# Expert gates of a mixture layer: one product of 256 columns per token, sums added by VectorE, steps of eight tokens

## The reference, cut to what matters

```
expert_idx = take_along_axis(cand_idx, best_c)        # (T, 8, 16): first key * 128 + second key
gates = softmax(best_s)
u = take(expert_u, ib);  act = gelu(einsum('td,thkd->thk', xb, u))
w = gb * act
v = take(expert_v, ib);  out = einsum('thk,thkd->td', w, v)
```

## Time and profile before

| | |
|---|---|
| median of 3 runs | 3182.61 us (3180.1 to 3184.99) |
| the profiled execution | 3179.26 us, its span 3177.4 us |
| mean granted TensorE clock | 0.994 of full speed |
| TensorE busy | 3115.6 us (98%) |
| GpSimd busy | 2335.9 us (74%) |
| VectorE busy | 1830.0 us (58%) |
| ScalarE busy | 767.3 us (24%) |

### The profile page before, as it was taken

How to read it: one execution, slowest core, us unless ns; L and a number is a source line. 1 busy time by engine, 2 the same in 40 slices (tenths; PEclk the granted TensorE clock), 3 DMA queues, 4 the chain that set the end, 5 groups by cost and what they waited for, 6 DMA issues and landing times.

```text
span 3177.4 us, 41446 instructions
## 1 busy us (share of the span) xinstructions
PE 3115.6 (98%) x14250; PEld 2523.3 (79%) x14250; DVE 1830.0 (58%) x2659; ACT 767.3 (24%) x1253; POOL 2335.9 (74%) x1127
## 2 busy tenths in 40 slices
PE   8999999999999999999999999999999998899998
PEld 6788777788888888888888888888888775578886
DVE  6488645221255566665764266767676667776621
ACT  3244123220122222222323111111111255332201
POOL 6833654677776888888888788888888763278876
PEclk9999999999999999999999999999999999899999
DMA  3211211223322344344444666666666421022222
GB/s 143 93 51 50 100 66 53 79 99 119 108 96 95 130 182 174 144 156 176 173 169 172 235 190 189 190 191 186 185 185 188 144 78 45 27 90 96 99 92 73
DMA packets 245547, 405.71 MB, mean 128 GB/s; under 512 B 145600, under 2 KB 145728, under 8 KB 244160
## 3 DMA queue, kind: packets, MB, share of 16 engines
q1 hardware_dynamic: 224560, 331.68, 32.0%
q10 hardware_dynamic: 20880, 72.62, 5.9%
HBM read 335.04 MB, written 69.21 MB: 127 GB/s over the span
## 4 chain that ended last, share of the span: by engine, by line
PE 93%; DVE 4%; POOL 1%; issue 1%; ACT 1%; DMA 0%; POOLq 0%; SPq 0%; ACTq 0%; DVEq 0%
PE bank L598 23%; PE bank L600 23%; PE bank L599 23%; PE banks L598 2%; PE banks L600 2%; PE banks L599 2%; PE banks L747 1%; PE bank L812 1%; PE bank L713 1%; PE bank L711 1%; PE bank L712 1%; PE bank L895 1%; PE banks L896 1%; PE bank L896 1%; PE banks L895 1%
## 5 line engine op out<-in xcount | busy, mean ns | idle before, releaser
L500 POOL TENSOR_TENSOR w_hi<-w_raw,ones 128x1024 fp32r<-128x1024 f32 x492 | 956.0, 1943 | 731.9 <-PE bank L600 581.3
L502 POOL TENSOR_TENSOR w_lo<-w_raw,w_hi 128x1024 fp32r<-128x1024 f32 x492 | 1231.6, 2503 | 38.6
L598 PE MATMUL bank<-h_hi,w_hi 128*128 128x512 f32 x2176 | 864.1, 397 | 9.6 <-DVE h_lo L1878 7.0
L600 PE MATMUL bank<-h_hi,w_lo 128*128 128x512 f32 x2176 | 848.1, 390 | 0.0
L599 PE MATMUL bank<-h_lo,w_hi 128*128 128x512 f32 x2176 | 847.2, 389 | 0.0
L598 PEld LDWEIGHTS bank<-h_hi,w_hi 128*128 128x128 f32 x2176 | 408.8, 188 | 105.0 <-DVE h_lo L1878 13.9
L600 PEld LDWEIGHTS bank<-h_hi,w_lo 128*128 128x128 f32 x2176 | 408.4, 188 | 86.8
L599 PEld LDWEIGHTS bank<-h_lo,w_hi 128*128 128x128 f32 x2176 | 409.0, 188 | 82.3 <-issue 2.4
L2343 DVE TENSOR_TENSOR ew_lo<-expert_w,ew_hi 128x512 fp32r<-128x512 f32 x128 | 249.1, 1985 | 182.3 <-ACT ew_hi L1585 178.5
L598 PE MATMUL bank<-ew_hi,w_hi 128*128 128x512 f32 x768 | 303.2, 395 | 0.0
L600 PE MATMUL bank<-ew_hi,w_lo 128*128 128x512 f32 x768 | 303.0, 395 | 0.0
(11 more groups left out here) (443 smaller groups left out, 4390.6 us busy)
## 6 DMA issues: line engine op xcount, KB each, us to landing
w_raw<-weights SPq DMA_DIRECT2D x494, 512.0 KB, 3.2
acts<-act_out_stage ACTq DMA_DIRECT2D x128, 256.0 KB, 2.6
gates<-gate_stage ACTq DMA_DIRECT2D x8, 4096.0 KB, 13.2
acts_in<-acts SPq DMA_DIRECT2D x128, 256.0 KB, 4.3
gates_in<-gates SPq DMA_DIRECT2D x128, 256.0 KB, 4.6
resid<-x SPq DMA_DIRECT2D x4, 512.0 KB, 7.9
resid<-x ACTq DMA_DIRECT2D x4, 512.0 KB, 7.9
out<-final SPq DMA_DIRECT2D x3, 512.0 KB, 2.7
```

Source lines behind the costliest of these rows:

```text
L500: nc.gpsimd.tensor_tensor(w_hi[:, pair, :], w_raw[:, slot, :], one_col.to_broadcast((P, 1024)), ALU.mult).then_inc(hi_split, 1)
L502: nc.gpsimd.tensor_tensor(w_lo[:, pair, :], w_raw[:, slot, :], f32(w_hi[:, pair, :]), ALU.subtract).then_inc(split_done, 1)
L598: mm(out_, hi, rhs_hi, start=first, stop=False)
L600: return mm(out_, lo, rhs_hi, start=False, stop=last)
```

## The change

The two parts of the gate lie side by side in one tile, `hot1[..., 0, :]` and `hot1[..., 1, :]`, and a token is **one product of 256 columns** in place of two of 128. Its two halves of the result are no longer added by TensorE. ScalarE copies the first half to a new tile `gate_part`, VectorE adds the second half, which it reads from the bank, and writes the sum to `gate_stage` (`gates_summed`, L2301 of the changed kernel).

A batch of 4 tokens now needs two banks, so a **step is 2 batches, 8 tokens** (`HOTS` = 2): 64 steps, 8 to a lot, 16 to a block. `LOT_TILES` now gives the tiles of each single step, one or two. In the first three blocks the steps of one tile are step 3, 11 and 14 of the 16. In the last block the row of steps is 1 1 2 1 1 2 1 2, then 2 1 1 2 1 1 1 1. The number of tiles among the steps is 108 as before. VectorE's pieces of the choice are cut anew: five rows in parts 1 and 2, four and two rows in parts 4 and 5, `choose` in halves in parts 6 and 7, `places` in part 9, `picked` in 10 and 12, `chosen_gates` in 13.

```
-LOT_TILES = (4, 4, 4, 4, 3, 3, 3, 2)
+LOT_TILES = ((2, 2, 2, 1, 2, 2, 2, 2), (2, 2, 2, 1, 2, 2, 1, 2)) * 3 + ((1, 1, 2, 1, 1, 2, 1, 2), (2, 1, 1, 2, 1, 1, 1, 1))
-HOTS = 4
+HOTS = 2
...
-    hot1 = place("hot1", [P, HOTS, TOKENS_PER_BATCH, NKEYS], A0 + 56 * KB, F32R)
-    hot1_lo = place("hot1_lo", [P, HOTS, TOKENS_PER_BATCH, NKEYS], A0 + 24 * KB, F32R)
+    hot1 = place("hot1", [P, HOTS, TOKENS_PER_BATCH, 2, NKEYS], A0 + 56 * KB, F32R)
...
+    gate_part = place("gate_part", [P, HOTS, TOKENS_PER_BATCH, NKEYS], S1 + 12 * KB + 64)
...
         for step in range(TT * LOTS * STEPS):
-            n = LOT_TILES[step // STEPS]
-            early = min(n, 3)
-            splits(early)
-            tile += early
+            n = LOT_TILES[step // STEPS][step % STEPS]
+            splits(n)
+            tile += n
             for p in range(HOTS if step + 1 < TT * LOTS * STEPS else 0):
                 gate_batch(step + 1, p)
-                if p == 0:
-                    splits(n - early)
-                    tile += n - early
...
                 for t in range(TOKENS_PER_BATCH):
-                    mm(bank[2 + p][:, t * P:t * P + P], hot2[:, p, t, :], hot1[:, p, t, :], start=t == 0, stop=False)
-                    ins = mm(bank[2 + p][:, t * P:t * P + P], hot2[:, p, t, :], hot1_lo[:, p, t, :],
-                             start=False, stop=t == TOKENS_PER_BATCH - 1)
+                    of = (t % 2) * 2 * NKEYS
+                    ins = mm(bank[2 + 2 * p + t // 2][:, of:of + 2 * NKEYS], hot2[:, p, t, :], hot1[:, p, t].rearrange("p a k -> p (a k)"),
+                             start=t % 2 == 0, stop=t % 2 == 1)
                 ins.then_inc(batch_done, 1)
...
-                fn_at(stage[:, :, bass.ds(t0, TOKENS_PER_BATCH)].rearrange("p k t -> p t k"),
-                      bank[2 + p][:].rearrange("p (t k) -> p t k", k=NKEYS), ACT.Copy).then_inc(gate_read, 1)
+                fn(gate_part[:, p], gate_sums[p][:, :, 0, :], ACT.Copy).then_inc(gate_copied, 1)
...
+        def gates_summed(step):
+
+            if step % STEPS == 0 and step:
+                dve.wait_ge(gates_out, 16 * (step // STEPS))
+            for p in range(HOTS):
+                first = (step % STEPS * HOTS + p) * TOKENS_PER_BATCH
+                dve.wait_ge(gate_copied, c.due(gate_copied))
+                tt_(stage[:, :, first:first + TOKENS_PER_BATCH].rearrange("p k t -> p t k"), gate_sums[p][:, :, 1, :], gate_part[:, p],
+                    ALU.add).then_inc(gate_read, 1)
...
             one_hots(step + 1)
+            gates_summed(step)
             if tt + 1 < TT:
```

More of the change, by code:

```diff
@@ L274, in build @@
     bank += [df_banks[:, 0, :], df_banks[:, 1, :]]
-    bank += [nc.alloc_psum_tensor(f"bank{n}", [P, T], F32) for n in range(4, 8)]
+    banks45 = nc.alloc_psum_tensor("banks45", [P, 2, T], F32)
+    bank += [banks45[:, 0, :], banks45[:, 1, :]]
+    bank += [nc.alloc_psum_tensor(f"bank{n}", [P, T], F32) for n in range(6, 8)]
+    gate_sums = [pair[:].rearrange("p b (t part k) -> p (b t) part k", part=2, k=NKEYS) for pair in (df_banks, banks45)]
     gates = nc.dram_tensor("gates", (T // STAGED_TOKENS, NKEYS, NKEYS, STAGED_TOKENS), F32, kind="Internal").ap()
@@ L300, in build @@
         "hi_split", "split_done", "hot_gated"))
-    choices_here = sem("choices_here")
+    choices_here, gate_copied = (sem(n) for n in ("choices_here", "gate_copied"))
     tile_done, sq_used, lev_done, far_done, o_done = (sem(n) for n in (
@@ L515, in gate_batch @@
             gate = gates_t[:, first:first + TOKENS_PER_BATCH]
-            nc.gpsimd.tensor_tensor(hot1[:, p], f32(hot1[:, p]), gate.unsqueeze(2).to_broadcast((P, TOKENS_PER_BATCH, NKEYS)),
-                                    ALU.mult).then_inc(hot_gated, 1)
+            nc.gpsimd.tensor_tensor(hot1[:, p, :, 0, :], f32(hot1[:, p, :, 0, :]),
+                                    gate.unsqueeze(2).to_broadcast((P, TOKENS_PER_BATCH, NKEYS)), ALU.mult).then_inc(hot_gated, 1)
         tile = START["experts"]
@@ L903, in _, with mixed, twos @@
         tiles_fm(LEAD_TILES - TURN_AT, h_hi, h_lo, acc_read_act)
-        for lot in range(TT * LOTS):
[L906 to L917, removed]
-            else:
-                c.repeat(STEPS - 1, lambda i: mixed())
-                mixed(0, next_choices)
-        tiles_fm(NKEYS - LEAD_TILES - LOT_BATCHES // HOTS * sum(LOT_TILES), h_hi, h_lo, acc_read_act)
+        def mixed(n, first, next_choices=0):
+            gate_batches()
+            for k in range(n):
+                p = (first + k) % 2
+                pe.wait_ge(acc_read_act, c.due(acc_read_act, 1, back=2))
+                tile_fm(p, h_hi, h_lo, bank[p][:])
+                if k == 0 and next_choices:
+                    turn(next_choices)
+        def twos(n, first):
+            c.repeat(n, lambda i: mixed(2, first))
+        tile = LEAD_TILES
+        for lot in range(TT * LOTS):
+            first = tile % 2
+            if lot >= LOTS * (TT - 1):
+                for n in LOT_TILES[lot]:
+                    mixed(n, tile % 2)
+                    tile += n
+                continue
+            twos(3, first)
+            mixed(1, first)
+            if lot % LOTS == LOTS - 1:
+                twos(2, 1 - first)
+                mixed(1, 1 - first, (lot + 1) // LOTS)
+                mixed(2, first)
+            else:
+                twos(4, 1 - first)
+            tile += sum(LOT_TILES[lot])
+        tiles_fm(NKEYS - tile, h_hi, h_lo, acc_read_act)
         pe.wait_ge(gate_read, c.due(gate_read, 0))
@@ L1556, in _ @@
         for lot in range(TT * LOTS):
[L1557 to L1563, removed]
+            for step in range(STEPS):
+                gate_batches()
+                if step == STEPS - 1:
                     act.wait_ge(gate_read, c.due(gate_read, LOT_BATCHES))
@@ L1566, in mixed @@
                                   stage[:].rearrange("p a t -> p (a t)")).then_inc(gates_out, 16)
-                for k in range(n):
-                    key_act(i * n + (key + k), (i * n + k) % 2)
-                    if share and k == 1:
+                for k in range(LOT_TILES[lot][step]):
+                    key_act(key, key % 2)
+                    key += 1
+                    if lot % LOTS == 1 and lot + 1 < TT * LOTS and step == 0 and k == 1:
                         shares()
[L1571 to L1575, removed]
+        c.due(gates_out, 16 * TT * LOTS)
         key_acts(key, NKEYS - key - 2)
@@ L2222, in choose_halves, with choose @@
             dve.wait_ge(dve_step, c.due(dve_step, 3))
-        def choose():
-            best16([(cand[:, h, :], best_s[:, h, :], best_u[:, h * TOPK:h * TOPK + TOPK]) for h in range(PEER_HEADS)])
+        def choose(first=0, end=PEER_HEADS):
+            best16([(cand[:, h, :], best_s[:, h, :], best_u[:, h * TOPK:h * TOPK + TOPK]) for h in range(first, end)])
+            if end < PEER_HEADS:
+                return
             ve.tensor_copy(denom[:, 0, :], best_s[:, :, 0]).then_inc(dve_step, 1)
@@ L2320, in _ @@
             one_hots(step + 1)
+            gates_summed(step)
             if tt + 1 < TT:
[L2322 to L2326, removed]
+                if part in (1, 2, 4, 5):
+                    choose_halves(tt + 1, *{1: (0, 5), 2: (5, 10), 4: (10, 14), 5: (14, 16)}[part])
+                elif part == 6:
+                    choose(0, PEER_HEADS // 2)
+                elif part == 7:
+                    choose(PEER_HEADS // 2)
+                elif part == 9:
                     places(tt + 1)
-                    picked(tt + 1, 0)
-                elif part == STEPS + 2:
-                    picked(tt + 1, 1)
+                elif part in (10, 12):
+                    picked(tt + 1, part // 12)
+                elif part == 13:
                     chosen_gates()
+        gates_summed(TT * per_block - 1)
         def second_layer(i):
```

12 lines of the change are left out of this document (4 added, 8 removed).

## The result

The changed kernel takes **3201.61 us** (median of 4 runs, 3200.56 to 3203.05), the kernel before beside it 3181.36 us (4 runs, 3179.73 to 3184.99): a ratio of 1.0062, 95% interval 1.0045 to 1.008. It is slower by 20 us. The forecast was 3193.

A forecast was written before the change was run, and what follows sets the result against it. TensorE was taken to bound the gate steps, GpSimd next. Products -54.4, stalls +57.9 and clock +7 gave +10.5 us on the profiled 3179.3, 3189.8; on the median 3193 us, range 3170 to 3214.

The forecast's parts named there:

- one-tile steps wait for GpSimd's split: Steps of one tile: TensorE waits for GpSimd's split behind one-hots and two multiplications, 2.9 us a step.
- The gate products: On TensorE, 512 products of 256 columns: 64 x 0.95 = 60.8 us in place of 115.2, saving 54.4.
- the rival of columns at two cycles: Gate products on TensorE: 256 columns at the slow rate cost 113 us, time near 3215 us; chance 0.05.
- VectorE's sum: VectorE's added sum with its scattered write: 1.14 us each, spaced 1.06, between 0.69 and 1.26.
- Rival 1: VectorE's scattered write costs nothing, sum 0.69 us: 3173 us without clock falls, 3180 with four; chance 0.19.
- The stalls: TensorE's waits over the gate steps: 39.0 us in three blocks, 17.4 and 1.5 in the last, 57.9 in all.
- Behind part 7 ... 2.5: Behind part 7 of the choice in each of three blocks, one-hots some 5 us late: TensorE waits 2.5 us.
- the transfer of `gate_stage`: Last block's second step: VectorE first waits for this transfer, landing 13.3 us after issue; costs 1.5 us.
- The bank waits of 1.2 us: Step 3 and behind `picked` in step 11: VectorE's second sum is late for TensorE's bank, 1.2 us each.
- The clock: TensorE's clock falls behind its gaps: 4 falls taken, 7 us, from none to 18, 0 to 31 us.
- a clock below 1.00 in many windows: Sign that the forecast is wrong: TensorE's granted clock below 1.00 in many windows.
- The likeliest case: Waits and priced write, with no to many clock falls: the forecast of 3193 us; chance 0.55.

The follow-up runs named there:

- e_ahead: Changed kernel, but behind a one-tile step GpSimd splits the next step's first tile before its two gate multiplications; 3141.88 us, 0.9873 of the kernel before.
- e_flat: Changed kernel, but VectorE's sum writes 512 neighbouring elements of gate_stage instead of 512 lying 64 elements apart; 3183.76 us, 1.0016 of the kernel before.
- e_ports: Changed kernel plus 24 small VectorE copies behind the last one-hots, 12 reading on-chip memory and 12 a bank; 3201.14 us in one run.
- e_fill: Changed kernel, but TensorE multiplies constant tiles where it stood idle, the waits staying as long; 3180.7 us, 0.9997 of the kernel before.
- e_narrow: Changed kernel's steps, but two products of 128 columns per token, added by TensorE and copied by ScalarE, without VectorE's sum; 3214.6 us, 1.0105 of the kernel before.

## Why the prediction was right, and where it was not

**The outcome and its sign** came from the mechanism named: one-tile steps wait for GpSimd's split behind two multiplications. The 15 waits for `w_lo` are all at the places listed, none behind a step of two tiles. The chain was priced at 10.27 us from a step's first product to the late tile; in the last block it is 1669.08 - 1658.93 = 10.15, and the step is 2.87 us longer where I had 2.9. `e_ahead` shows that it was the order.

**The gate products**: 64 x 0.95 forecast, 64 x 0.97 measured; 53.1 us saved in place of 54.4. The stationary tile and 256 columns pass together, the rival of columns at two cycles is out.

**VectorE's sum**: 1.14 forecast, 1.09 measured, all of the surplus from the write (`e_flat`). By the Trainium skill (VectorE: DVE Perf Modes, the 1x mode) it should have stayed at 0.69; the measurement decides against that reading. The other page (SBUF — State Buffer, Specifications), with its penalty for accesses that each go to another 16-byte line, agrees with it in sign; the price of 0.40 us for 512 scattered elements is the runs'. Rival 1 is `e_flat` itself: 3183.8 between its two groups, where I had 3180 with four falls. It would not have been faster than before.

**The stalls** were put at 57.9 us and are 46 as listed, 49 with the starts. Two terms failed. "Behind part 7 ... 2.5" did not occur in any block, 7.5 us: I priced the second half of `choose` at 9.1 us, half of 9.36 and an end of 4.44 from the earlier trace rows; it took 6.0, because its end took 1.0:

```profile
1151.62 0.17 DVE L2226 COPY denom<-best_s 128x8 f32<-128x8 f32 x1
1151.70 0.63 DVE L2230 TENSOR_SCALAR place_u<-best_u 128x128 uint32<-128x128 uint32 x4
1152.36 0.29 DVE L2232 TENSOR_TENSOR best_s<-best_s,denom 128x128 f32<-128x128 f32 x1
```

The copy is 0.17 here and 1.14 in the earlier trace rows, at the same size. Before, it ended with a GpSimd split; here GpSimd was idle from 1151.34 to 1152.38, and `e_ports` shows the rule. I had taken a coincidence for a price. The other is the transfer of `gate_stage` at the second step of the last block, 1.5 us: issued at 1622.05, it had landed when VectorE came to its sum at 1635.98, straight behind the one-hots, since the step ahead had itself been stretched by its wait and fall of the clock, to 15.97 us from 11.86. In `e_ahead`, where that step takes 11.90, VectorE waited 2.96 us for it and TensorE 2.4. The bank waits of 1.2 us, behind step 3 and step 11 of each block, came as 0.2 and 2.0: that their sum held is luck.

**The clock** is the term that was mis-sized: "4 falls, 7 us", and measured eleven falls, 23 us by the windows and 21 by `e_fill`. I chose four because the stretches between the gaps were dense; density did not protect them. Had I let the clock fall at each of the 15 gaps that came, at 1.7 us, I would have had 25. Of the prediction's own signs of being wrong, "a clock below 1.00 in many windows" is the one that came.

The errors had opposite signs, -9 for the stalls and +16 for the clock, +1 for the products: 10.5 became some 20. The likeliest case was the right one, its time 8.6 us low; the range held it because it reached up to the rivals.

## What to carry to other kernels

When steps are made smaller, read each engine's program again for what now stands behind a wait: an instruction that was early because four others stood ahead of it becomes late when only one does, and to move one line may be worth more than the change. Price a standstill of an engine that sets the time with what the clock does behind it: here 49 us of waits cost 21 to 23 more, so that a wait cost nearly half as much again as its length, while the 9 us of waits of `e_ahead` left the clock at 1.00. And compare the same instruction's duration at several places before it goes into a sum.

## What the runs showed of the hardware

- A VectorE copy of 8 elements from on-chip memory to on-chip memory lasts 0.15 us or until GpSimd's running instruction ends, up to 2.3 us; one that reads a bank lasted 0.15 to 0.16 in 12 of 12. The Trainium skill (Advanced Engine Details and Errata, VectorE Performance Modes) says that VectorE's second port is shared with GpSimd and that GpSimd's instructions and VectorE's in the modes that use both ports block each other; the run agrees, and here the copy waited to the end of the running instruction.
- A standstill of 2.2 to 2.9 us between dense tiles may take TensorE's clock to its lower level or not: 11 of 15 did here, 11 in `e_ports` but not all at the same places, 8 of the same 15 in the trace of `e_flat`, and 5 of 15 with 0.9 to 1.5 us in that of `e_narrow`. In `e_ahead` eleven bank waits, up to 2.2 us, passed without one. What decides between equal gaps stays open.
- A product of 256 columns whose stationary tile is new passes in 0.12 us, one of 128 in 0.11: the second half of the columns is nearly free.
